# A decoder layer on one core: products in token-chunk order, with the norms placed between them and their squares summed on VectorE

## The reference

```python
x = x + 0.5 * swiglu(rmsnorm(x, g_ffn1), w1_gate, w1_up, w1_down)   # 1024 -> 2816 -> 1024
h = rmsnorm(x, g_mix)
z = h @ w_in          # mLSTM q,k,v,i,f,o | attention q,k,v | two branch gates
# mLSTM branch -> y_m, dilated attention branch -> y_a
x = x + (sigmoid(gm) * y_m + sigmoid(ga) * y_a) @ w_out
x = x + 0.5 * swiglu(rmsnorm(x, g_ffn2), w2_gate, w2_up, w2_down)
y = rmsnorm(x, g_final)

def rmsnorm(x, g):    # over the 1024 features of a token
    return x * rsqrt(mean(x * x) + EPS) * g
```

## Time and profile before

| | us |
|---|---|
| three runs, median | 2993.76 |
| lowest and highest of them | 2988.28, 2995.37 |
| profiled execution, span from first to last instruction | 2991.6 |
| PE busy in it (matmuls) | 2805.8 |
| DVE, POOL, ACT busy in it | 957.0, 815.0, 429.8 |

### The profile page before, as it was taken

How to read it: one execution, slowest core, us unless ns; L and a number is a source line. 1 busy time by engine, 2 the same in 40 slices (tenths; PEclk the granted TensorE clock), 3 DMA queues, 4 the chain that set the end, 5 groups by cost and what they waited for, 6 DMA issues and landing times. The chain is left out here.

```text
span 2991.6 us, 40056 instructions
## 1 busy us (share of the span) xinstructions
PE 2805.8 (94%) x16508; PEld 2649.3 (89%) x16508; DVE 957.0 (32%) x1963; ACT 429.8 (14%) x859; POOL 815.0 (27%) x202
## 2 busy tenths in 40 slices
PE   5999999999979999999979988789889999999997
PEld 3999999999969999999967773489789999999995
DVE  6222222222262100330036655461432222222224
ACT  3010101001030011001123422120310001010002
POOL 3233333333323233333200002005123333333330
PEclk8999999999999999999978868899999999999998
DMA  4011111111113322223154225552011111111101
GB/s 146 29 42 43 55 42 42 42 42 42 43 42 128 104 88 87 91 88 120 45 183 113 89 83 221 190 172 81 15 43 42 42 42 42 42 52 46 42 0 60
DMA packets 86219, 221.63 MB, mean 74 GB/s; under 512 B 10532, under 2 KB 64220, under 8 KB 71164
## 3 DMA queue, kind: packets, MB, share of 16 engines
q1 hardware_dynamic: 61512, 191.02, 18.8%
q10 hardware_dynamic: 24628, 29.50, 2.8%
HBM read 174.61 MB, written 45.89 MB: 74 GB/s over the span
## 5 line engine op out<-in xcount | busy, mean ns | idle before, releaser
L707 PE MATMUL ps<-h_hi,whi 128*128 128x384 f32 (+1 forms) x3072 | 1007.0, 328 | 25.6 <-DVE act_lo L1452 25.6
L709 PE MATMUL ps<-h_hi,wlo 128*128 128x384 f32 (+1 forms) x3072 | 1006.5, 328 | 0.0
L708 PE MATMUL ps<-h_lo,whi 128*128 128x384 f32 (+1 forms) x3072 | 1006.1, 327 | 0.0
L657 POOL TENSOR_TENSOR whi<-raw,con 128x2048 fp32r<-128x2048 f32 x99 | 357.1, 3607 | 2080.1 <-PEq L693 1535.4
L707 PEld LDWEIGHTS ps<-h_hi,whi 128*128 128x128 f32 x3072 | 578.2, 188 | 26.5 <-DVE act_lo L1452 26.3
L708 PEld LDWEIGHTS ps<-h_lo,whi 128*128 128x128 f32 x3072 | 578.1, 188 | 0.1
L709 PEld LDWEIGHTS ps<-h_hi,wlo 128*128 128x128 f32 x3072 | 577.9, 188 | 0.0
L659 POOL TENSOR_TENSOR wlo<-raw,whi 128x2048 fp32r<-128x2048 f32 x99 | 457.8, 4624 | 7.8
L1439 DVE SCALAR_TENSOR_TENSOR x<-ps,x 128x384 f32<-128x384 f32 (+1 forms) x528 | 282.6, 535 | 226.0 <-PE ps L677 224.9
L675 PE MATMUL ps<-act_hi,whi 128*128 128x384 f32 (+1 forms) x1056 | 346.1, 328 | 4.0 <-DVE x L1439 4.0
L677 PE MATMUL ps<-act_hi,wlo 128*128 128x384 f32 (+1 forms) x1056 | 345.2, 327 | 0.0
(11 more groups left out here) (197 smaller groups left out, 2488.6 us busy)
## 6 DMA issues: line engine op xcount, KB each, us to landing
raw<-stream SPq DMA_DIRECT2D x99, 1024.0 KB, 4.9
vc<-vc_in SPq DMA_DIRECT2D x8, 1170.0 KB, 5.6
kc<-kc_in SPq DMA_DIRECT2D x8, 1152.0 KB, 9.8
zgate<-stage ACTq DMA_DIRECT2D x16, 384.0 KB, 2.5
sgate<-zgate SPq DMA_DIRECT2D x16, 384.0 KB, 3.4
zqko<-stage ACTq DMA_DIRECT2D x12, 384.0 KB, 2.5
oc<-o_att SPq DMA_DIRECT2D x8, 396.0 KB, 6.0
va_out<-sva ACTq DMA_DIRECT2D x24, 130.0 KB, 1.8
```

What stands on the lines that cost most here:

```text
L657: pool.tensor_tensor(whi[:, j, :], raw[:, j, :], con[:, C_ONES:C_ONES + 1].to_broadcast([P, SLAB]), ALU.mult).then_inc(hi_split, 1)
L707: pe.matmul(out, w_hi, h_hi[:, k, a:a + w], start=(k == 0), stop=False)
L708: pe.matmul(out, w_hi, h_lo[:, k, a:a + w], start=False, stop=False)
L709: mm = pe.matmul(out, w_lo, h_hi[:, k, a:a + w], start=False, stop=(k == KT - 1))
```

## The change

Feed-forward iterations run by token chunk: pair units (c, j) = (0,0), (0,1), (1,0), (1,1), down-projection of chunk 0, units (2,0), (2,1), down-projections of chunks 1 and 2. The gate-row and value units of slabs 0 and 1 run three token tiles at a time, chunk by chunk; the output projection runs slab 0 for all chunks and then slabs 1 to 3 chunk by chunk. A norm has twelve groups g = 3 n + c. ACT squares feature tile 0 into a sum `ssum` and the others into `sq`; DVE adds each of the seven to the sum; one ones-product per group follows, placed inside a pair unit, a down-projection or between units (`middle`). Roots, reciprocals, scalings and high and low parts of a chunk are placed between the accumulations, evictions or hidden units of the next one, on ACT and DVE alike. `slab_free` starts at 3 and is raised by the first matmul of a unit (`frees`). The last norm writes to a full-size `yst` in place of two buffers. The first chunk of x is loaded in two halves. The tables cost and sint are loaded after the last value store.

The core of the diff:

```diff
-SUM_BANK = (0, 2, 3)
-PAIRS_BEFORE = (0, PU_F, PU_FFN2, PU_FFN2 + 6 * FFN_ITERS)
+SUM_BANK = (4, 5, 6, 3, 0, 1, 0, 1, 2, 3, 0, 1)
...
+def value_units():
+    out = []
+    for c in range(NC):
+        out += [(-1, c)] + [(s, t) for s in (0, 1) for t in range(3 * c, 3 * c + 3)]
+    return out + [(s, t) for s in (2, 3, 4) for t in range(9)]
...
+def out_units():
+    return ([(0, c, dd) for c in range(NC) for dd in range(2)]
+            + [(s, c, dd) for c in range(NC) for s in (1, 2, 3) for dd in range(2)])
...
-            sp.dma_start(ch(x[:, :, :], 0), ch(xT, 0)).then_inc(x_in[0], 16)
+            for k in (0, 4):
+                sp.dma_start(ch(x[:, k:k + 4, :], 0), ch(xT[:, k:k + 4, :], 0)).then_inc(x_in[3 * k // 4], 16)
...
-                    sp.dma_start(y_out[:, k, a:a + w], htmp[:, q % 2, 0:w]).then_inc(y_stored[q % 2], 16)
+                    sp.dma_start(y_out[:, k, a:a + w], yst[:, k, a:a + w]).then_inc(y_stored[q % 2], 16)
...
+            def norm_sum(g):
+                w = CHUNKS[g % 3][1]
+                pe.wait_ge(sq_added, 7 * g + 7)
+                pe.matmul(bank(SUM_BANK[g], w), ones, ssum[:, g % 2, 0:w], start=True, stop=True).then_inc(sum_full, 1)
...
+                    pair(0, 0, frees=(n == 1 or not first),
+                         middle=(lambda: norm_sum(g0 + 2)) if first and n == 1 else None)
+                    pe.wait_ge(slab_ready, 3 * i + (s0 + 2))
+                    if first and n == 1:
+                        pe.wait_ge(std_ready, g0 + 3)
+                    pair(0, 1, middle=(lambda: norm_sum(1)) if first and n == 0 else None)
+                    pair(1, 0)
+                    pair(1, 1, middle=(lambda: norm_sum(2)) if first and n == 0 else None)
+                    pe.wait_ge(slab_ready, 3 * i + (s0 + 3))
+                    if first and n == 0:
+                        pe.wait_ge(std_ready, 3)
+                    down(0)
+                    pair(2, 0, middle=sum_early if last else None)
+                    if last:
+                        pe.wait_ge(std_ready, g1 + 1)
+                    pair(2, 1, frees=True)
+                    down(1, frees=True)
+                    down(2, middle=sum_next if last else None)
...
+                         frees=((s, t) in ((0, 6), (1, 6), (2, 0), (3, 0), (4, 0)))).then_inc(acc_full, 1)
+                if (s, t) == (0, 2):
+                    norm_sum(5)
...
+                    frees=((s, c, dd) in ((1, 0, 0), (2, 2, 0), (3, 2, 0)))).then_inc(acc_full, 1)
+                if (s, dd) == (1, 0) and c > 0:
+                    norm_sum(6 + c - 1)
...
-            dve.sem_inc(slab_free, 2)
+            dve.sem_inc(slab_free, 3)
...
+            def add_square(g, k):
+                w = CHUNKS[g % 3][1]
+                m = 7 * g + k - 1
+                dve.wait_ge(sq_ready, 8 * g + k + 1)
+                if k > 1:
+                    dve.wait_ge(sq_added, m)
+                dve.tensor_tensor(ssum[:, g % 2, 0:w], ssum[:, g % 2, 0:w], sq[:, m % 2, 0:w], ALU.add).then_inc(sq_added, 1)
...
+                if n == 0:
+                    for k in range(1, KT):
+                        add_square(0, k)
+                    inverse(0)
+                    for m in range(KT):
+                        norm_step(0, m)
+                    for k in range(1, KT):
+                        add_square(1, k)
+                    hidden(0, 0)
+                    inverse(1)
+                    for m in range(KT):
+                        norm_step(1, m)
+                    hidden(0, 1)
+                    for k in range(1, KT):
+                        add_square(2, k)
+                    hidden(0, 2)
+                    inverse(2)
+                    for m in range(KT):
+                        norm_step(2, m)
+                    hidden(0, 3)
...
+                for d in range(KT):
+                    accumulate(i, 0, d)
+                    if d > 1:
+                        add_square(g1, d - 1)
+                add_square(g1, KT - 1)
+                inverse(g1)
+                for m in range(KT):
+                    norm_step(g1, m)
+                hidden(i, 4)
+                hidden(i, 5)
+                for d in range(KT):
+                    accumulate(i, 1, d)
+                    if d > 1:
+                        add_square(g1 + 1, d - 1)
+                add_square(g1 + 1, KT - 1)
+                for d in range(KT):
+                    accumulate(i, 2, d)
+                    if d > 1:
+                        add_square(g1 + 2, d - 1)
+                    if d == 3:
+                        inverse(g1 + 1)
+                    if d >= 4:
+                        norm_step(g1 + 1, 2 * (d - 4))
+                        norm_step(g1 + 1, 2 * (d - 4) + 1)
+                add_square(g1 + 2, KT - 1)
...
+                if s > 0:
+                    add_square(6 + c, d - 1)
+                    if c > 0 and d == 2:
+                        inverse(6 + c - 1)
+                    if c > 0 and 3 <= d < 7:
+                        norm_step(6 + c - 1, 2 * (d - 3))
+                        norm_step(6 + c - 1, 2 * (d - 3) + 1)
+                    if d == KT - 1:
+                        add_square(6 + c, KT - 1)
```

More of the change, by code:

```diff
@@ L384, in program @@
         v_stored = [sem(f"v_stored{i}") for i in range(2)]
-        x_in = [sem(f"x_in{i}") for i in range(3)]
+        x_in = [sem(f"x_in{i}") for i in range(4)]
         yT_ready = sem("yT_ready")
@@ L666, in _, with products @@
             ident = con[:, C_ID:C_ID + P]
-            def products(out, parts, nk, h_before=None):
+            def products(out, parts, nk, h_before=None, frees=False):
                 for k in range(nk):
@@ L674, in products @@
                     w_hi, w_lo, x_hi, x_lo = parts(k)
-                    pe.matmul(out, w_hi, x_hi, start=(k == 0), stop=False)
+                    mm = pe.matmul(out, w_hi, x_hi, start=(k == 0), stop=False)
+                    if k == 0 and frees:
+                        mm.then_inc(slab_free, 1)
                     pe.matmul(out, w_hi, x_lo, start=False, stop=False)
@@ L678, in products, with pair_unit @@
                 return last
[L680 to L695, removed]
+            def norm_sum(g):
+                w = CHUNKS[g % 3][1]
+                pe.wait_ge(sq_added, 7 * g + 7)
+                pe.matmul(bank(SUM_BANK[g], w), ones, ssum[:, g % 2, 0:w], start=True, stop=True).then_inc(sum_full, 1)
+            def pair_unit(j, c, unit, par, h_before=None, frees=False, middle=None):
                 a, w = CHUNKS[c]
@@ L702, in pair_unit @@
                         pe.wait_ge(h_ready, h_before + k + 1)
+                    if k == KT // 2 and middle is not None:
+                        middle()
                     for half, full in ((0, gate_full), (1, up_full)):
@@ L706, in pair_unit @@
                         out = bank(2 * par + half, w)
-                        pe.matmul(out, w_hi, h_hi[:, k, a:a + w], start=(k == 0), stop=False)
+                        mm = pe.matmul(out, w_hi, h_hi[:, k, a:a + w], start=(k == 0), stop=False)
+                        if k == 0 and half == 0 and frees:
+                            mm.then_inc(slab_free, 1)
                         pe.matmul(out, w_hi, h_lo[:, k, a:a + w], start=False, stop=False)
@@ L755, in _ @@
                 j = (S_V + s) % 3
+                a = min(t * P, TOK - P)
                 pe.wait_ge(slab_ready, S_V + s + 1)
[L757 to L768 removed]
@@ L781, in _ @@
                     for c in range(NC):
[L782 to L784 removed]
+                        pair_unit(j % 3, c, 18 * i + (PU_F + 3 * j + c), (3 * j + c) % 2, frees=(c == 0))
             pe.wait_ge(gM_ready, 1)
@@ new lines, in ffn @@
+                downs(0)
+                with dve.Fori(1, FFN_ITERS - 1) as i:
+                    for k in range(4):
+                        hidden(i, k)
+                    downs(i)
+                i = FFN_ITERS - 1
+                for k in range(4):
+                    hidden(i, k)
+                dve.wait_ge(acc_free, 24 * i + (au + 4))
+                for d in range(KT):
+                    accumulate(i, 0, d)
+                    if d > 1:
+                        add_square(g1, d - 1)
```

516 lines of the change are left out of this document (284 added, 232 removed).

## The result

The changed kernel takes **2945.2 us** (median of four runs, 2943.6 to 2946.9) against 2994.2 us for the kernel before, four runs beside it: ratio 0.984, interval 0.983 to 0.985. The forecast was 2932 with a range from 2893 to 2960.

What follows compares the result with a forecast made beforehand. TensorE (PE) sets the pace, so only its idling at four places, 195 us of norms and waits, can be won: 7.1 + 14.5 + 23.1 + 16.6 = 61.3 off the 2993.8 median gives 2932 us, range 2893 to 2960.

Steps and rivals of the forecast that it cites:

- Place 1: Kernel start to end of feed-forward iteration 0: forecast 125.7 us against 132.8, saving 7.1.
- place 2: Last iteration of FFN 1 plus value products: forecast 244.9 us against 259.4, saving 14.5.
- place 3: Output projection plus first iteration of FFN 2: forecast 189.3 us against 212.4, saving 23.1.
- place 4: Last iteration of FFN 2 to the end: forecast 94.0 us against 110.6, saving 16.6.
- the first pause: FFN 1's last iteration: PE, out of banks at 60.9 us, waits till 78.3 for hidden units and accumulations behind norm instructions.
- The second: Before the second value group: PE waits 10 us, from 105.4 to 115.4, for a value eviction to free a bank.
- The loops: Feed-forward iterations between the places: forecast to stay at 71.4 us each, with PE busy throughout.
- "slower" rival: Feed-forward loops: PE's four banks run out waiting for DVE's hidden-part chain, over 3.1 us lost per iteration; 3034 us, chance 0.04.
- The projection stage: Projections between values and attention, 477.1 us before: the prediction gave no term for a change there.
- "The port costs less": Rival: shorter port turns or splits falling elsewhere, saving 117 us; 2876 us, anything to 2909 counting; chance 0.20.
- "The gain is eaten": Rival: stalls at 60.9, 105 and 100.7 each ten to fifteen us longer through serial chains; 2967 us, chance 0.12.
- the two long pauses: PE idle some 17 us in FFN 1's last iteration and 18 us inside FFN 2's first unit.

Runs made afterwards that it cites:

- run 1: Changed kernel with POOL splitting only 64 of 2048 columns in most feed-forward and value slabs: place 2 219.9, place 3 171.3, span 2899.8 us.
- run 6: Changed kernel with the third slab's release moved from pair unit (0,0) to (0,1): loop iterations 71.84 and 71.72, span 2954.7 us.
- run 7: Changed kernel with chunk 2's pair units first in the looped feed-forward iterations: 71.49 us an iteration, span 2938.1 us.
- run 8: Changed kernel with PE's loop over gate-and-up slabs written out: stage between values and attention 477.1, span 2945.2 us.
- runs 1 to 3: Changed kernel, then kernel before, with most weight splitting cut; changed kernel with third norm's operands in PSUM, whole split: spans 2899.8, 2992.1, 2927.9 us.

## Why the prediction was right, and where it was off

**The places: right.** Place 1 was forecast at 125.7 and took 126.4, place 2 244.9 and 243.9, place 3 189.3 and 190.9, place 4 94.0 and 93.6. The mechanism that carried the forecast, two instructions of DVE passing for each split of a slab, holds in the timelines, and run 1 gives its price in places 2 and 3. The prediction counted norms and waits together, 195 us in the four places. Apart, the whole gain is in the first: the ones-products' busy time fell by 66.5 us (78.1 to 11.6; 63 were counted), while PE's idle time in the places stayed near where it was, 104.4 and 108.8. In places 2 and 3 run 1 shows what kept it there: the additions and norm steps that met the splits. No run takes the change into its parts, so what the new order and what the sums on DVE are worth by themselves is not shown.

**Inside place 1** the sum of the squares was not ready at 13 to 17 but at 20, as the last two additions waited under the first slab's split. It moved little, as the prediction said, for the slab itself was done at 19.6. PE's pause before the first accumulations was forecast from 81.9 to 89.8 and came from 83.1 to 90.7.

**Inside place 2** the first pause ran from 61.4 to 78.9 after the place's start, forecast 60.9 to 78.3. The second was forecast as one of 10 us before the second value group; it came as 2.4 and 5.1 before the gate rows and the first value units. The step that failed: the banks of those units are freed by the last accumulations of FFN 1, and these stand on DVE behind chunk 1's norm, the first behind its reciprocal, which waited 2.03 us for the root, and the next behind norm steps under a split:

```profile
865.44 2.55 DVE L1500 RECIPROCAL rstd<-rstd 128x384 f32<-128x384 f32 x1 [2.03 <-ACT rstd L1122]
873.06 4.88 DVE L1522 TENSOR_TENSOR h_lo<-htmp,h_hi 128x384 fp32r<-128x384 f32 x1
```

I had let only the value evictions wait.

**Inside place 3** PE stopped at 102.2 for 18.4 us, forecast 100.7 for 18 to 19. **Place 4:** no slab, no waits under splits.

**The loops: the term that was mis-sized.** "The loops between stay at 71.4 us" was taken from the count of matmuls and one pace for each width. They took 71.84 and 71.72, 6.5 us over 18 iterations (646.56 and 645.44 against 642.70 and 642.78), and run 6 clears the release and run 7 shows that the order of the units moves it: a 384-column matmul has no one pace, and mostly takes 0.177 us here where the prediction had 0.175. The prediction had named a longer loop as what would prove it wrong, but for a wait on DVE's chain; PE never waited, so the "slower" rival has no part in it.

**The projection stage: missed.** Nothing in the change touches it, so it was put at nothing. It took 4.5 us more, and run 8 shows that the loop's back edge is the cause. With 1.1 in the attention stage and 0.9 in the places this makes the 13 us between the forecast's 61.3 and the 48.0 of the profiled executions. The range was wide enough for them, but not because they had been thought of.

**The rivals.** "The port costs less" falls with runs 1 to 3: in places 2 and 3 the forecast and this rival lie 19.8 and 18.5 us apart, and the splits cost 24.0 and 19.6. "The gain is eaten" by longer pauses: the two long pauses were not longer. Part of the gain that the change could have had is eaten by the port, and that was the forecast itself.

## What to carry to other kernels

Before work is moved onto DVE beside POOL's own, count the instructions that read two SBUF tiles: here the port took half of the change's worth in one place and a third in another, and one operand in an idle PSUM bank brought much of it back. Judge an edit by the window of its stage, not by the total: two edits of 5 and 8 us each vanished in the attention stage of their one execution, and counted in full once put together. And a stage that an edit does not touch still needs a term when it loops or changes width.

## What the runs showed of the hardware that was not expected

- Matmuls of 384 columns run at 0.173, 0.175 or 0.177 us each until the width changes; another order of the units moved the mean, but one and the same change of width was followed by all three. The 320-column ones kept to 0.147 (3.52 us for 24).
- The same loop of 864 matmuls paused 0.9 to 1.4 us around its back edge in one program and not at all in another; where one pause was 3.4 to 4.2 us, with 6.8 us at 1.2 GHz next to it, the loop cost 10 us in all.
- When the clock falls after a stage begins is not fixed: in these profiles it fell 3.8 to 7.5 us after the start of the attention stage, which took 512 to 529 us, and the five longest are the five with a fall inside 4.1.
